# The prompt's delta rule with its inverses' levels in 32x32 and 64x64 blocks

## The reference

```
A   = strict_lower(beta * (k k^T) * decay)          # within a chunk
sol = solve(I + A, [beta*v, beta*k*exp(gc)])        # u, w
att = (q k^T) * decay
# from chunk to chunk, with the state S (128x128 per head):
v_new = u - w S
o     = (q*exp(gc)) S + att v_new
S     = S*exp(g_last) + (k*exp(g_last - gc))^T v_new
```

## Time and profile before

| | us |
|---|---|
| median of 3 runs | 1769.63 (1769.43 to 1771.33) |
| the profiled execution's own time | 1769.2 |
| its span, first to last instruction | 1766.9 |
| TensorE busy in the span | 1730.6 (98%) |
| VectorE, ScalarE, GpSimd busy | 1123.8, 468.7, 253.7 |
| prompt's delta rule, 265.96 to 362.46 | 96.5 |

### The profile page before, as it was taken

How to read it: one execution, slowest core, us unless ns; L and a number is a source line. 1 busy time by engine, 2 the same in 40 slices (tenths; PEclk the granted TensorE clock), 3 DMA queues, 4 the chain that set the end, 5 groups by cost and what they waited for, 6 DMA issues and landing times. The chain is left out here.

```text
span 1766.9 us, 21908 instructions
## 1 busy us (share of the span) xinstructions
PE 1730.6 (98%) x7699; PEld 1353.9 (77%) x7699; DVE 1123.8 (64%) x2212; ACT 468.7 (27%) x1108; POOL 253.7 (14%) x540
## 2 busy tenths in 40 slices
PE   8999999998989999999999999999899999999999
PEld 5777779985767777777777777777677777777777
DVE  4766778859776666763337655567766676642365
ACT  2433406633332222220005101113322222200051
POOL 0111116644210000000110000002100000001100
PEclk9999999999999999999999999999999999999999
DMA  4232220024112222232121222221122222322211
GB/s 152 72 112 85 80 60 13 5 105 155 48 59 81 75 72 84 83 130 102 66 89 45 96 72 82 83 62 48 48 83 84 72 72 84 127 90 91 73 61 54
DMA packets 45642, 139.34 MB, mean 79 GB/s; under 512 B 4944, under 2 KB 12240, under 8 KB 45536
## 3 DMA queue, kind: packets, MB, share of 16 engines
q1 hardware_dynamic: 42864, 133.36, 22.9%
q10 hardware_dynamic: 2672, 4.61, 0.8%
HBM read 129.63 MB, written 8.31 MB: 78 GB/s over the span
## 5 line engine op out<-in xcount | busy, mean ns | idle before, releaser
L274 PE MATMUL bank<-z,ring 128*128 128x288 f32 x1952 | 507.2, 407 | 7.4 <-DVE z L392 2.8
L274 PEld LDWEIGHTS bank<-z,ring 128*128 128x128 f32 x1952 | 370.0, 190 | 113.7 <-issue 5.1
L274 PE MATMUL bank<-x,ring 128*128 128x288 f32 x1632 | 428.5, 409 | 9.9 <-DMA x<-in_x 4.7
L274 PEld LDWEIGHTS bank<-x,ring 128*128 128x128 f32 x1632 | 310.5, 191 | 100.8 <-issue 7.3
L2081 DVE SCALAR_TENSOR_TENSOR scratch<-scratch 128x592 f32<-128x592 f32 x176 | 146.3, 832 | 25.5 <-ACT scratch L2025 23.8
L274 PE MATMUL bank<-y,ring 128*128 128x288 f32 x616 | 156.6, 406 | 2.0 <-DVE x L1842 2.0
L274 PEld LDWEIGHTS bank<-y,ring 128*128 128x128 f32 x616 | 117.0, 190 | 34.7 <-issue 2.4
L274 PE MATMUL bank<-big,ring 128*128 128x288 f32 x536 | 135.1, 407 | 2.7 <-issue 1.1
L274 PEld LDWEIGHTS bank<-big,ring 128*128 128x128 f32 x536 | 101.4, 190 | 32.3 <-issue 3.4
L2025 ACT ACTIVATE scratch<-scratch 128x592 f32<-128x592 f32 x88 | 69.4, 789 | 91.0 <-DVE scratch L2055 89.5
L2115 POOL COPY scratch<-scratch 128x2 f32<-128x2 f32 x88 | 26.4, 300 | 466.0 <-ACT scratch L2011 466.0
(11 more groups left out here) (374 smaller groups left out, 2377.5 us busy)
## 6 DMA issues: line engine op xcount, KB each, us to landing
ring<-in_w_up SPq DMA_DIRECT2D x88, 512.0 KB, 3.5
ring<-in_w_scin SPq DMA_DIRECT2D x24, 512.0 KB, 3.5
ring<-in_w_qkv SPq DMA_DIRECT2D x21, 512.0 KB, 3.5
ring<-in_w_down SPq DMA_DIRECT2D x12, 704.0 KB, 4.2
scratch<-in_w_down SPq DMA_DIRECT2D x12, 704.0 KB, 5.4
ring<-in_w_z SPq DMA_DIRECT2D x8, 512.0 KB, 3.5
big<-in_st_S SPq DMA_DIRECT2D x16, 256.0 KB, 5.9
out_dn_S_sample<-big SPq DMA_DIRECT2D x16, 256.0 KB, 2.6
```

The lines of the kernel that those rows point to most:

```text
L274: last = pe.matmul(bank[:, 0:HALF], w[:, k * P:(k + 1) * P], rhs(k), start=start and k == 0, stop=k == self.depth - 1, skip_group_check=no ...
```

## The change

Each level forms only the blocks that it needs. In level one TensorE multiplies 32x32 blocks (two per head for Y, three per head for the corrections), in level two 64x64 blocks (one per head each). A block lies at its own partitions (`quad`), and all eight heads' blocks of one kind lie side by side in one bank (`by_head`). Beta is applied by one VectorE operation for all heads of a row of blocks; no mask is needed. Since the blocks of T are zero before, the corrections are copied into T and not subtracted: VectorE copies the two that the second level reads, ScalarE the two that are read only by the new values' product.

Banks are no longer tied to heads: four "pairs" and four "groups", whose roles turn from chunk to chunk (`bank_roles`). Transpositions, state products, outputs and updates run in groups of four heads and signal once per group; the new values are copied for two heads at a time. TensorE's order becomes: keys and queries, values transposed, Y of level one, keys transposed, corrections of level one, state products of heads 0 to 3, Y of level two, state products of heads 4 to 7, correction of level two, last outputs transposed, new values, outputs and updates. The first products of a chunk and of the samples no longer wait for the outputs to be squared (in the samples the last four heads still wait for the state or the squares).

On ScalarE the next chunk's decays come behind the new values, as do the samples' exponentials in the last chunk; EG comes behind the first copy into T (in chunk 0 it stays first). VectorE takes over the scaling of the outputs of heads 0 to 3, in one operation between the two groups of state updates, and gates in two operations per chunk. GpSimd forms the last column of the decays ahead of the normalising. The samples' state loads wait for a group of heads each.

The new lines and what stays around them, indentation cut; removed lines are left out of the longer pieces (they stand in the listing above). What is left out replaces `BANK` by `SBANK` in Samples and adapts counts.

```diff
+YS0 = VNEW.rearrange("p h t -> p (h t)")[:, 0:H * BL].rearrange("p (h t) -> p h t", h=H)
+YS1 = VNEW.rearrange("p h t -> p (h t)")[:, H * BL:3 * H * BL].rearrange("p (h t) -> p h t", h=H)
+HG = H // 2
+GROUPS = (range(0, HG), range(HG, H))
+
+def quad(r, n=1):
+return slice(BL * r, BL * (r + n))
+
+def by_head(bank, part, cols):
+
+return BANK[bank][part, 0:H * cols].rearrange("p (h t) -> p h t", h=H)
+
+def bank_roles(c):
+
+pairs, groups = [0, 1, 2, 3], [4, 5, 6, 7]
+for _ in range(c):
+    pairs, groups = ([groups[2], groups[3], pairs[0], pairs[2]],
+                     [groups[0], groups[1], pairs[1], pairs[3]])
+return pairs, groups
...
+def turn_pe(self, pe, bank, group, rows, done):
+    for h in GROUPS[group]:
+        last = pe.transpose(BANK[bank][:, h % HG * P:(h % HG + 1) * P], rows(h), IDENT[:])
+    last.then_inc(done, 1)
+
+def state_rows_pe(self, pe, c, bank, group):
+    for h in GROUPS[group]:
+        last = pe.matmul(BANK[bank][:, h % HG * P:(h % HG + 1) * P], BIG[:, 3 * h, self.col(c)], S[:, h, :],
+                         start=True, stop=True)
+    last.then_inc(self.ks, 1)
...
+        pairs, groups = bank_roles(c)
         for h in range(H):
+            last = pe.matmul(BANK[pairs[h // 2]][:, h % 2 * 256:(h % 2 + 1) * 256], BIG[:, 3 * h, cols],
+                             BIG[:, 3 * h:3 * h + 2, cols], start=True, stop=True)
+            if h % 2:
+                last.then_inc(self.kq, 1)
+        for group in range(2):
             if c:
+                pe.wait_ge(self.s_out, (c - 1) * H + (group + 1) * HG)
+            self.turn_pe(pe, groups[group], group, lambda h: BIG[:, 3 * h + 2, cols], self.by_tok)
+        pe.wait_ge(self.inited, NBL * (c + 1) + c)
+        pe.wait_ge(self.att, H * (c + 1))
         for h in range(H):
+            for r in (0, 2):
+                last = pe.matmul(by_head(pairs[r // 2], quad(r + 1), BL)[:, h, :],
+                                 KA[quad(r), h, 0, quad(r + 1)], T[quad(r), h, 0, quad(r)], start=True,
+                                 stop=True)
+        last.then_inc(self.level, 1)
+        for group in range(2):
+            if c:
+                pe.wait_ge(self.o_sq, (c - 1) * H + (group + 1) * HG)
+            self.turn_pe(pe, groups[2 + group], group, lambda h: BIG[:, 3 * h, cols], self.by_tok)
+        pe.wait_ge(self.ymask, 3 * c + 2)
         for h in range(H):
+            for r in (1, 3):
+                bank = pairs[2 + r // 2]
+                if r == 1:
+                    pe.matmul(by_head(bank, quad(r), BL)[:, h, :], T[quad(r), h, 1, quad(r)],
+                              YS0[quad(r), h, :], start=True, stop=True)
+                last = pe.matmul(by_head(bank, quad(r - 1), BL)[:, h, :], YS0[quad(r), h, :],
+                                 T[quad(r), h, 1, quad(r)], start=True, stop=True)
+        last.then_inc(self.level, 1)
+        self.state_rows_pe(pe, c, pairs[1], 0)
+        pe.wait_ge(self.t_dve, 2 * c + 1)
         for h in range(H):
+            last = pe.matmul(by_head(pairs[0], quad(2, 2), 2 * BL)[:, h, :], KA[quad(0, 2), h, 0, quad(2, 2)],
+                             T[quad(0, 2), h, 0, quad(0, 2)], start=True, stop=True)
+        last.then_inc(self.level, 1)
+        pe.wait_ge(self.t_dve, 2 * c + 2)
+        self.state_rows_pe(pe, c, pairs[3], 1)
+        pe.wait_ge(self.ymask, 3 * c + 3)
         for h in range(H):
+            last = pe.matmul(by_head(pairs[0], quad(0, 2), 2 * BL)[:, h, :], YS1[quad(2, 2), h, :],
+                             T[quad(2, 2), h, 1, quad(2, 2)], start=True, stop=True)
+        last.then_inc(self.level, 1)
         if c:
             pe.wait_ge(self.scaled, c)
+            for group in range(2):
+                pe.wait_ge(self.tok, 4 * c + group + 1)
+                self.turn_pe(pe, groups[group], group, lambda h: OT[:, h, :], self.ot)
+        pe.wait_ge(self.t_act, 2 * c + 2)
         for h in range(H):
+            if h % 2 == 0 and h < HG:
+                pe.wait_ge(self.tok, 4 * c + 3 + h // 2)
+            pe.wait_ge(self.r, c * H + h + 1)
+            bank = (groups[2], groups[3], pairs[0], pairs[2])[h // 2]
+            last = pe.matmul(BANK[bank][:, h % 2 * P:(h % 2 + 1) * P], T[:, h, 1, :], YS[:, h, :], start=True,
+                             stop=True)
+            if h % 2:
+                last.then_inc(self.v, 1)
+        pe.wait_ge(self.qe, c + 1)
+        for group in range(2):
+            out, update = BANK[pairs[1 + 2 * group]], BANK[groups[group]]
             if c:
+                pe.wait_ge(self.gated, 2 * (c - 1) + group + 1)
+            for h in GROUPS[group]:
+                at = slice(h % HG * P, (h % HG + 1) * P)
+                pe.wait_ge(self.vnew, 4 * c + h // 2 + 1)
+                pe.matmul(out[:, at], QE[:, h, :], S[:, h, :], start=True, stop=False)
+                pe.matmul(out[:, at], KA[:, h, 1, :], VNEW[:, h, :], start=False, stop=True)
+                last = pe.matmul(update[:, at], KTOK[:, h, :], VNEW[:, h, :], start=True, stop=True)
+            last.then_inc(self.os, 1)
...
+def right_side_dve(self, dve, c, bank, group):
+    dve.wait_ge(self.ks, 2 * c + group + 1)
+    dve.wait_ge(self.tok, 4 * c + group + 1)
+    for h in GROUPS[group]:
+        dve.scalar_tensor_tensor(out=YS[:, h, :], in0=BANK[bank][:, h % HG * P:(h % HG + 1) * P],
+                                 scalar=TOKS[:, c, 2, h:h + 1], in1=VTOK[:, h, :], op0=ALU.mult,
+                                 op1=ALU.add).then_inc(self.r, 1)
+
+def gate_dve(self, dve, c, bank, group, ready):
+    heads = slice(group * HG, (group + 1) * HG)
+    dve.wait_ge(*ready)
+    dve.scalar_tensor_tensor(out=BIG[:, 1:QKV_T:3, self.col(c)][:, heads], scalar=norm_g,
+                             in0=BANK[bank][:].rearrange("p (h t) -> p h t", h=HG),
+                             in1=Z[:, heads, self.col(c)], op0=ALU.mult, op1=ALU.mult
+                             ).then_inc(self.gated, 1)
...
+        dve.wait_ge(self.level, 4 * c + 1)
+        for r in (1, 3):
+            dve.tensor_tensor(YS0[quad(r)], by_head(pairs[r // 2], quad(r), BL),
+                              TOKS[quad(r), c, 3, :].unsqueeze(2).to_broadcast([BL, H, BL]),
+                              ALU.mult).then_inc(self.ymask, 1)
+        dve.wait_ge(self.level, 4 * c + 2)
+        dve.tensor_copy(T[quad(1), :, 0, quad(0)], by_head(pairs[2], quad(1), BL)).then_inc(self.t_dve, 1)
+        dve.tensor_copy(T[quad(2), :, 1, quad(3)], by_head(pairs[3], quad(2), BL)).then_inc(self.t_dve, 1)
+        self.right_side_dve(dve, c, pairs[1], 0)
+        dve.wait_ge(self.level, 4 * c + 3)
+        dve.tensor_tensor(YS1[quad(2, 2)], by_head(pairs[0], quad(2, 2), 2 * BL),
+                          TOKS[quad(2, 2), c, 3, :].unsqueeze(2).to_broadcast([2 * BL, H, 2 * BL]),
+                          ALU.mult).then_inc(self.ymask, 1)
+        self.right_side_dve(dve, c, pairs[3], 1)
         if c:
+            for group in range(2):
+                self.gate_dve(dve, c - 1, groups[group], group, (self.ot, 2 * (c - 1) + group + 1))
+        for group in range(2):
+            dve.wait_ge(self.os, 2 * c + group + 1)
+            for h in GROUPS[group]:
+                dve.scalar_tensor_tensor(out=S[:, h, :], in0=S[:, h, :], scalar=EG[:, h, CH - 1:CH],
+                                         in1=BANK[groups[group]][:, h % HG * P:(h % HG + 1) * P],
+                                         op0=ALU.mult, op1=ALU.add).then_inc(self.s_out, 1)
+            if group == 0:
+                dve.tensor_tensor(OT[:, 0:HG, :], BANK[pairs[1]][:].rearrange("p (h t) -> p h t", h=HG),
+                                  NRM[:, c, 1:2 * HG:2].unsqueeze(2).to_broadcast([P, HG, P]), ALU.mult
+                                  ).then_inc(self.o_out, 1)
...
+        if c == 0:
+            act.activation(EG, Y[:, :, self.col(c)], ACT.Exp).then_inc(self.eg, 1)
+        else:
+            act.wait_ge(self.o_sq, c * H)
+        for group in range(2):
+            act.wait_ge(self.by_tok, 4 * c + group + 1)
+            for h in GROUPS[group]:
+                last = act.activation(VTOK[:, h, :], BANK[groups[group]][:, h % HG * P:(h % HG + 1) * P],
+                                      ACT.Copy, scale=TOKS[:, c, 1, h:h + 1])
+            last.then_inc(self.tok, 1)
+        act.wait_ge(self.last, c + 1)
+        for group in range(2):
+            act.wait_ge(self.by_tok, 4 * c + group + 3)
+            for h in GROUPS[group]:
+                last = act.activation(KTOK[:, h, :], BANK[groups[2 + group]][:, h % HG * P:(h % HG + 1) * P],
+                                      ACT.Copy, scale=LAST_DEC[:, h:h + 1])
+            last.then_inc(self.tok, 1)
+        act.wait_ge(self.level, 4 * c + 2)
+        act.activation(T[quad(0), :, 1, quad(1)], by_head(pairs[2], quad(0), BL), ACT.Copy
+                       ).then_inc(self.t_act, 1)
+        if c:
+            act.wait_ge(self.s_out, c * H)
```

(70 more changed lines are left out.)

125 lines of the change are left out of this document (32 added, 93 removed).

## The result

| | before | after |
|---|---|---|
| median, us (same chip) | 1769.93 | 1751.49 |
| the profiled execution's own time | 1769.2 | 1752.5 |
| its span | 1766.9 | 1749.1 |
| four chunks of the prompt's rule | 96.50 | 77.78 |
| from there to the samples' first state product | 7.09 | 7.42 |

The ratio is 0.9894 with the interval [0.988, 0.9907]: by the medians 18.4 us faster, where 6.0 were forecast. One of the four executions of the changed kernel took 3027 us at a mean granted clock of 0.556; it is in the median above and not in the ratio, and the other three have the median 1750.47.

A forecast was written before the change was run, and what follows sets the result against it. TensorE's instruction stream was taken as the bound: 7.5 us off the four chunks less 1.5 lost at the rule's end, 6.0 off 1769.2, gives 1763.2; the median lies 0.4 above, 1763.6 us, range 1758 to 1770.

The forecast's parts named there:

- the price of a 32x32 product: TensorE, both level-one steps: 40 products a chunk at 0.09 us each, 3.60 us (2.56 to 4.68).
- A, the floor: 32-column blocks take as long as 64-column ones: 4.3 us more, 1767.9 us; chance 0.20 together with D.
- B, the hop that costs: Each 32x32 block pays 0.10 us for changing array position: 16 us more, 1779.6 us; chance 0.12.
- C, the overlap: Blocks at different array rows and two banks overlap, 0.064 us or below: 4.2 us more off, 1759.4 us; chance 0.08.
- D: TensorE waits at four hand-overs a chunk, 0.4 us each, 6.4 us, all the gain; chance 0.20 together with A.
- The range: Whole kernel: 1758 us (0.06 us a block, no shape changes) to 1770 us (a hop of 0.04 us).
- Changes of shape: TensorE switching between full-size and small products: 0.245 us a round trip, four per chunk, 0.98 us.
- Waits: TensorE: Y for KA 0.57 us (chunk 0: 0.23), last correction for YS1 0.2, chunk 0's new values 0.88.
- The end of the rule: After the last chunk, ScalarE's squares and 16 copies delay the samples' state products: 1.5 us lost.
- Covers: Slack hiding moved work; smallest is 1.2 us, between GpSimd's argument for the next decays and ScalarE's need of it.
- E: The time at which TensorE has issued a chunk's last product and goes on to the next chunk.

The follow-up runs named there:

- the first two experiments: Changed kernel with 32x32 blocks issued place by place: 1755.14 us, 0.9925; changed kernel with unused products at a fourth and a second place: 1750.54 us, 0.9898.
- the kernel run again: The changed kernel without an edit, beside other runs of the kernel before: 1751.31 us against 1769.09, 0.9896.
- the step further: Changed kernel with Y waiting for KA head by head and chunk 0's products with the zero state left out: 1747.76 us against 1768.58, 0.9882.

## Why the prediction was wrong

The direction and the reason were right (TensorE's stream is the bound, and what leaves it counts), the size was a third of the result.

**The failed step is the price of a 32x32 product.** I bounded it from below by "a line of 0.83 ns a column and 5 ns fixed; at 32 columns 0.032 us, so 0.064 a product", and took 0.09. That line comes from records of which each uses the place of the one before, or the whole array. For that case it held: 0.033 us a record at one place. But the change puts neighbours at two and three places, and those run side by side, at 0.016 and 0.011 us a record. Forty products cost 0.50 + 0.51 = 1.0 us a chunk, 2.6 less than forecast: 10.3 of the 12.4 us by which the rule was missed. Of the 2.6, 1.0 is the step from the line's 0.064 up to 0.09, and 1.6 is the overlap. The failed step is thus to add up all 80 records as if they came one after the other. The listing told which places alternate: 16 records at each, 0.51 us a step by the line's own 0.032, is the bound from below, and it is what was measured. The Trainium skill, TensorEngine Tiling (Array Packing), Key Properties, says that different tiles load weights and multiply in parallel. I took from that section only the sentence on the drain; the first two experiments agree with the other one, 0.033 us a record at one place against 0.016 and less.

**The rivals.** A, the floor, falls: 32-column records at one place are 0.033 us apart, not 0.058. B, the hop that costs, falls: the hop is what gains. C, the overlap, was the mechanism, with a chance of 0.08 and a price two to three times too high (0.064 a product is 0.032 a record, against 0.016 and 0.011); neither of its conditions, rows of their own and two banks, is needed. D falls: TensorE waits a quarter of a microsecond in each of chunks 1 to 3.

**The range.** Its low end is summed wrongly: 0.06 us a block (4.8 us off) and no changes of shape (3.9 us off) give 1763.6 - 4.8 - 3.9 = 1754.9 and not 1758. The result lies below that, too.

**Changes of shape.** The remainder of chunk 1 after 15.11 + 1.87 of stream, 1.0 of blocks and 0.25 of wait is 1.2 us, against 0.98 for four round trips. It is a remainder and not a measurement of them: 0.1 us of it are the 64x64 records, 0.0615 us apart here where the forecast had 0.0585.

**Waits.** Forecast were 0.57 us for KA and 0.2 for YS1; measured 0.25 and none. VectorE's order of time in chunk 1 shows why:

```profile
284.50 1.12 DVE L686 SCALAR_TENSOR_TENSOR scratch<-scratch,bank 128x128 f32<-128x128 f32 x4 [0.96 <-PE bank L634]
285.54 3.36 DVE L662 SCALAR_TENSOR_TENSOR scratch<-bank,token_norms,scratch 128x256 f32<-128x256 f32 x8
```

Four updates take 1.04 us, 0.26 each, and KA 0.42. The 0.33 us that I took from L596 was busy time divided by count, where VectorE kept step with a product and a transposition of TensorE, 0.22 + 0.11 us. It was the producer's pace. In chunk 0 the new values wait 0.68 us, where 0.88 was forecast. All this is worth 2.0 us.

**The end of the rule.** Forecast was a loss of 1.5 us, measured 0.33. ScalarE's order of time:

```profile
341.90 0.37 ACT L750 ACTIVATE scratch<-bank,token_norms 128x128 f32<-128x128 f32 x1 [1.64 <-DVE ring L690]
...
343.28 0.38 ACT L749 ACTIVATE ring<-bank,token_norms 128x128 f32<-128x128 f32 x1
...
345.65 0.39 ACT L1047 ACTIVATE scratch<-bank,token_norms 64x128 f32<-64x128 f32 x1
```

With E = 342.71 the squares run from E - 0.81 to E + 2.94 (forecast E - 0.4 to E + 3.95): four lone squares take 343.28 - 341.90 = 1.38, 0.35 each and not 0.41, and the four with copies 345.65 - 343.28 = 2.37, 0.59 each and not 0.67; the sixteen copies that follow are 0.25 apart, not 0.265. The chain is the one described, 1.2 us shorter than summed.

**Covers.** The smallest one held, though barely: the next decays' argument is ready at 298.5 and ScalarE starts on it at 298.86, 0.35 us later where I had 1.2.

Sum over the rule, from the 6.0 forecast: 10.3 (blocks) + 2.0 (waits) - 0.9 (shapes) + 1.2 (end) gives 18.6, measured 18.39. Outside the rule the profiled execution started it 1.0 us earlier than the one before (264.93; the kernel run again starts it at 266.22), and was 1.6 us longer behind it (below).

## What to carry to other kernels

Small products at different places of the array cost a fraction of the same products at one place, so their order decides their price: alternate places from one instruction to the next, and bound their cost by the records of the fullest place and not by all of them. Busy time divided by count, of an engine that keeps step with another one, is the other one's pace; take it where the engine runs from a queue of finished work. What a shorter stream wins has to be covered by the copies that feed it: two moves of a few operations, one on ScalarE and one on VectorE, took back over half and all of the gain, the second in the main by the clock.

## What the runs showed of the hardware

- At the 2.4 GHz level 32x32 fp32 records start 0.033 us apart at one place, 0.016 at two, 0.011 at three and about 0.01 at four (64 records within 0.68 us); two 64x64 ones start together, in the time of one. The places may share rows of the array, and the bank that they write.
- A wait of 1.7 us amid small blocks was followed in three chunks of four by a fall of the granted clock to the 1.2 GHz level, which cost more than the wait. It isn't shown what decides: the fourth chunk kept its clock.
- The work behind the rule, from the samples' first state product to the end, takes 1398.97 us where it took 1397.35, and 1398.5 in the run again and in the step further; with the exponentials moved in the kernel before it takes 1397.4. In the profiles of the changed kernel, stretches behind the rule have a lower granted clock, as the first one here (and 0.91 from 460 to 480), where the kernel before has 1.00 throughout from 340 to 500:

```profile
400.00:420.00 20.00, 19.70 (x76) 14.87 (x76) 17.36 (x40) 2.15 (x5) 2.54 (x3) 0.93 0.36 131
400.00:420.00 20.00, 17.50 (x51) 8.80 (x52) 18.52 (x32) 9.82 (x39) 14.24 (x13) 0.91 0.57 213
400.00:420.00 20.00, 16.35 (x66) 11.89 (x65) 18.26 (x44) 1.71 (x4) 3.54 (x4) 1.00 0.55 199
```

The small blocks don't decide this. The second line is of the kernel before with the exponentials moved, which has none of them; the third is of the blocks ordered by place, which has them all, and whose work behind the rule takes 1397.4 us. Nor do such stretches decide the time: with the exponentials ahead of the new values there are two (0.91 from 400 to 420 and from 480 to 500), and the work behind the rule takes 1397.5 us; with every small block twice there is one, and it takes 1399.7. What makes the 1.6 us is open.
